# Computing neighbouring output tiles in pairs, with their matmuls in alternating PSUM banks, in a transformer forward pass on one core

## The reference

```python
def conv_ffn(h, w_up, conv_w, conv_b, w_down):
    u = h @ w_up                      # 1024 -> 2 x 2816
    up = jnp.pad(u, ((0, 0), (CONV_W - 1, 0), (0, 0)))
    c = conv_b + sum(up[:, j:j + Tp] * conv_w[j] for j in range(CONV_W))
    gate, val = jnp.split(c, 2, axis=-1)
    return (jax.nn.silu(gate) * val) @ w_down

def sq_relu_mlp(hn, w1, w2):          # 1024 -> 4096 -> 1024
    return jnp.square(jax.nn.relu(hn @ w1)) @ w2
```

## Time and profile before

| what | value |
|---|---|
| median of 3 runs | 1442.1 us (1436.69 to 1442.25) |
| the profiled execution: span | 1441.2 us |
| TensorE busy | 1380.6 us (96%), 10268 matmuls |
| VectorE busy | 925.0 us (64%) |
| ScalarE busy | 662.0 us (46%) |
| GpSimd busy | 471.5 us (33%) |
| mean granted TensorE clock | 0.934 |
| share of the chain that ended last on TensorE | 88% |

### The profile page before, as it was taken

The page is one execution under the profiler, slowest core; times in us unless marked ns, Lnnn a source line. Parts: engine busy times, 40 slices in busy tenths (PEclk is TensorE's granted clock), DMA queues, the critical chain, the costliest instruction groups (busy, mean ns, idle before and its releaser), DMA issues.

```text
span 1441.2 us, 29845 instructions
## 1 busy us (share of the span) xinstructions
PE 1380.6 (96%) x10268; PEld 1311.5 (91%) x10268; DVE 925.0 (64%) x1574; ACT 662.0 (46%) x1100; POOL 471.5 (33%) x479
## 2 busy tenths in 40 slices
PE   6899999999999898999999999999999899999997
PEld 5796999999999767999998899999999886999997
DVE  4587479996656665799955587565554663655542
ACT  3334345554443363465643445454434453444432
POOL 4020135553102312355521023278411000488322
PEclk9995799999999867999999999999999986999999
DMA  5740146556554201566565655666667440566662
GB/s 139 226 137 0 55 143 175 173 169 183 170 151 143 74 1 52 146 193 179 172 197 186 198 146 159 177 181 183 183 184 187 119 125 1 147 194 184 193 187 75
DMA packets 404187, 212.09 MB, mean 147 GB/s; under 512 B 21320, under 2 KB 398424, under 8 KB 403968
## 3 DMA queue, kind: packets, MB, share of 16 engines
q1 hardware_dynamic: 402176, 204.36, 49.3%
q0 software_dynamic: 880, 5.00, 1.0%
q10 hardware_dynamic: 1040, 1.50, 0.3%
HBM read 209.74 MB, written 3.23 MB: 148 GB/s over the span
## 4 chain that ended last, share of the span: by engine, by line
PE 88%; DVE 6%; POOL 2%; issue 2%; ACT 1%; DMA 1%; DVEq 0%; ACTq 0%; SPq 0%; POOLq 0%
PE bank L490 24%; PE bank L491 24%; PE bank L492 24%; PE bank L641 3%; PE bank L592 2%; DVE w_lo L1533 2%; PE bank L616 2%; PE bank L587 1%; PE bank L572 1%; PE bank L905 1%; PE bank L907 1%; PE bank L906 1%; DMA w_raw<-in_w_in_a_dram 1%; POOL acc L1386 1%; PE bank L935 0%
## 5 line engine op out<-in xcount | busy, mean ns | idle before, releaser
L1533 DVE TENSOR_TENSOR w_lo<-w_raw,w_hi 128x1024 fp32r<-128x1024 f32 x391 | 480.4, 1241 | 43.2 <-ACT w_hi L1074 42.6
L1074 ACT ACTIVATE w_hi<-w_raw 128x1024 fp32r<-128x1024 f32 x391 | 410.7, 1051 | 179.2 <-PE bank L492 143.6
L490 PE MATMUL bank<-xh,w_lo 128*128 128x256 f32 (+2 forms) x1640 | 477.2, 291 | 10.9 <-DVE xl L1590 7.1
L491 PE MATMUL bank<-xl,w_hi 128*128 128x256 f32 (+2 forms) x1640 | 470.8, 287 | 0.0
L492 PE MATMUL bank<-xh,w_hi 128*128 128x256 f32 (+2 forms) x1640 | 470.3, 287 | 0.0
L490 PE MATMUL bank<-wide_h,w_lo 128*128 128x256 f32 (+1 forms) x1324 | 381.6, 288 | 8.4 <-DVE wide_l L1601 2.0
L492 PE MATMUL bank<-wide_h,w_hi 128*128 128x256 f32 (+1 forms) x1324 | 378.6, 286 | 0.0
L491 PE MATMUL bank<-wide_l,w_hi 128*128 128x256 f32 (+1 forms) x1324 | 378.4, 286 | 0.0
L490 PEld LDWEIGHTS bank<-xh,w_lo 128*128 128x128 f32 x1640 | 313.4, 191 | 14.7 <-DVE xl L1590 8.3
L492 PEld LDWEIGHTS bank<-xh,w_hi 128*128 128x128 f32 x1640 | 313.5, 191 | 0.3
L491 PEld LDWEIGHTS bank<-xl,w_hi 128*128 128x128 f32 x1640 | 313.2, 191 | 0.3
(11 more groups left out here) (245 smaller groups left out, 1386.3 us busy)
## 6 DMA issues: line engine op xcount, KB each, us to landing
w_raw<-in_mlp_w_dram SPq DMA_DIRECT2D x256, 256.0 KB, 3.1
w_raw<-in_w_up_dram SPq DMA_DIRECT2D x176, 256.0 KB, 3.2
w_raw<-in_w_down_dram SPq DMA_DIRECT2D x64, 256.0 KB, 3.3
w_raw<-in_a_w_in_dram SPq DMA_DIRECT2D x64, 256.0 KB, 3.5
w_raw<-in_w_in_a_dram SPq DMA_DIRECT2D x34, 256.0 KB, 4.2
w_raw<-in_w_kv_b_dram SPq DMA_DIRECT2D x32, 256.0 KB, 3.2
w_raw<-in_a_w_out_dram SPq DMA_DIRECT2D x32, 256.0 KB, 3.1
w_raw<-in_w_down_dram SPq DMA_DIRECT2D x32, 192.0 KB, 4.0
```

Source lines behind the costliest of these rows:

```text
L490: pe.matmul(dst, lo, mov_h, start=first, stop=False)
L491: pe.matmul(dst, hi, mov_l, start=False, stop=False)
L1074: act.activation(w_hi[:, n % R, :], w_raw[:, n % R, :], ACT.Copy)\
L1533: dve.tensor_tensor(w_lo[:, n % R, :], w_raw[:, n % R, :], w_hi[:, n % R, :].bitcast(F32), ALU.subtract)\
```

## The change

In the wo, up and mlp stages PE takes two neighbouring tiles together (`two_products`): it waits for both banks and both weight blocks, and then issues for each k-slice L530, L532 and L534 for the one tile and the other in turn, so that two matmuls in a row write different banks. The same 48 matmuls as before are issued for two tiles; both `block_done` come with the last two of them. `stat_sums` goes to the middle of the first pair. On DVE, in loop stages with one block per tile, `prep(g)` comes ahead of `after(g)`. ACT, POOL and SP are left as they were.

```diff
--- before.py
+++ after.py
@@ -512,6 +512,28 @@
                                       k == 0, k == nk - 1)
                         return ins
                     step(s, i, g, b, body)
+
+            def two_products(s, i, g, mh, ml, t0, ready, nk, middle=None):
+
+                slots = [(s.n0 + g + t) % R for t in range(2)]
+                dsts = [stream[(s.t0 + g + t) % R][:, 0:T - t0] for t in range(2)]
+                for t in range(2):
+                    bank_free(s, i, g + t)
+                pe.wait_ge(S["lo_ready"], at(i, 4, s.n0 + g + 2))
+                for k in range(nk):
+                    if i is None:
+                        ready(k)
+                    if k == nk // 2 and middle is not None:
+                        middle()
+                    w = slice(k * P, (k + 1) * P)
+                    for slot, dst in zip(slots, dsts):
+                        pe.matmul(dst, w_lo[:, slot, w], mh(k), start=k == 0, stop=False)
+                    for slot, dst in zip(slots, dsts):
+                        pe.matmul(dst, w_hi[:, slot, w], ml(k), start=False, stop=False)
+                    for slot, dst in zip(slots, dsts):
+                        ins = pe.matmul(dst, w_hi[:, slot, w], mh(k), start=False, stop=k == nk - 1)
+                        if k == nk - 1:
+                            ins.then_inc(S["block_done"], 1)
 
             def from_x(s, t0=0):
                 base = SPLITS[s.name]
@@ -781,18 +803,25 @@
 
             def simple(name, src):
                 s = ST[name]
-                sweep(pe, s, lambda s, i, g: product(s, i, g, **src(s)), peel=True)
+
+                def pair(s, i, g):
+                    if g % 2 == 0:
+                        two_products(s, i, g, **src(s))
+                sweep(pe, s, pair, peel=True)
 
             def up(name, t0, first=None):
                 s = ST[name]
 
-                def group(s, i, g):
-                    product(s, i, g, **from_x(s, t0 if first is None else first))
+                def pair(s, i, g):
+                    middle = None
                     if i is None and g == 0:
-                        stat_sums(NORM[name], t0)
-                    if i is None and g == 1:
+                        middle = lambda: stat_sums(NORM[name], t0)
+                    if g % 2 == 0:
+                        two_products(s, i, g, middle=middle,
+                                     **from_x(s, t0 if first is None else first))
+                    if i is None and g == 0:
                         rb_sums(NORM[name], t0)
-                sweep(pe, s, group, peel=True)
+                sweep(pe, s, pair, peel=True)
 
             def down(name, t0, nk, stride, sem_, base):
                 s = ST[name]
@@ -1539,8 +1568,12 @@
                 def group(s, i, g):
                     for b in range(s.bpg - 1):
                         prep(s, i, g * s.bpg + b)
-                    after(s, i, g)
-                    prep(s, i, (g + 1) * s.bpg - 1)
+                    if s.loop and s.bpg == 1:
+                        prep(s, i, g)
+                        after(s, i, g)
+                    else:
+                        after(s, i, g)
+                        prep(s, i, (g + 1) * s.bpg - 1)
                     if late is not None:
                         late(s, i, g)
                 sweep(dve, ST[name], group, straight=straight)
```

## The result

The changed kernel takes **1559.1 us** (median of 4 executions, 1557.7 to 1563.2), the kernel before 1439.4 (4, 1432.8 to 1442.3). The ratio is 1.0838, 95% interval 1.0792 to 1.0885: slower by 8.4%. The forecast was 1544, the range 1505 to 1600. The profiled execution took 1559.77 us.

The account below looks back on a forecast made before the run. The prediction took PE to set the time before, and a DVE-ACT ring after the change. Terms 61 + 17 + 3 + 2 + 4 + 15 = 102 us on 1442 gave 1544 us, range 1505 to 1600.

Parts of the forecast that it names:

- The bank changes: PE's matmuls in pairs: alternating banks gain nothing; at most 6 ns a step, 25 us in all.
- The ring: Up and mlp stages: u, ACT's work, high half, DVE's low half, next u can't overlap; +61 us up, +17 mlp.
- Its Silu waits for a tap of tile 2 and starts 1.48 after u: Up stages, turn from g = 3: ACT's Silu delays the high half, making the turn 4.03 us.
- The clock: PE gaps in up0 and up1: half clock for 6.8 us behind one gap in four, +15 us.
- The starts: Starts of up0, up1 and mlp1: POOL's sum for `stat_sums` comes late; +1 us each, +3.
- The mlp stages: mlp0 and mlp1: ring turn of 3.11 us a tile against 2.84, 64 tiles, +17 us.
- The wo stages: wo stages: DVE already slower than PE, low half already in that ring; 0, at most +1 us a stage.
- 7 x 1: Rival without change: pipeline fills a tile later in each of seven stages, 1449 us; 4%.
- The ends: Ends of up0 and up1: last gated slice late for the down stage; 0 to +4 us each, +4 in all.
- the clock falls in most passes: Rival, up stages: gaps ahead of second pairs mostly bring half clock, near 1593 us; 15%.
- Faster: Rival, PE's matmuls: alternation cuts the step by 6 ns to 112 ns, 1417 us; 2%.
- No change: Rival: blocks ready anyway, needing ACT's high half ahead of cin; 1449 us; 4%.

Follow-up runs that it names:

- e5: e4 with each tile's three matmuls of a k-slice in a row in one bank; 1457.4 us, 1.0113 times before.
- e4: Changed kernel, pairs kept, with ScalarE making the next high half before its work on u, VectorE the next low half after its own; 1470.0 us, 1.0191 times before.
- e6: Kernel before, one tile at a time, with e4's order on both ScalarE and VectorE; 1413.7 us, 0.9820 times before.
- e9: e4 with the common wait kept, but all 24 matmuls of one tile ahead of the other's, each signalling its own end; 1428.7 us, 0.9912 times before.
- e2: Kernel before, one tile at a time, with only VectorE's new order, low half ahead of u(g); 1539.8 us, 1.0662 times before.
- e8: Changed kernel with eight extra unused matmuls ahead of each pass's second pair in up0 and up1; 1546.9 us, 1.0738 times before.
- e10: The same kernel as e6, timed again; 1420.0 us, 0.9849 times before.
- e1: Changed kernel with VectorE's order as in the kernel before, TensorE still taking pairs; 1664.6 us, 1.1538 times before.
- e3: Changed kernel, pairs and waits kept, with each tile's three matmuls of a k-slice in a row in one bank; 1550.5 us, 1.0758 times before.

## Why the prediction was right, and where it was off

The forecast was 15 us low, with the verdict and the main mechanism right. By its own steps:

**The bank changes gain nothing: right.** The test is e5 against e4, which differ in how often the bank changes and in nothing that PE waits for in mlp: the same time. There is a difference of 1.3 ns a step that the change does bring: four tiles of mlp take 11.36 us before, in e6 and in e9, which is 118.3 ns a matmul, and 11.23 in e4 and e5, 117.0. It comes with taking two tiles slice by slice, not with a bank change at each matmul, and is worth about 1 us in each mlp stage. Its cause isn't shown.

**The ring: right in kind.** The wait that it named is the one that grew, from 43 to 233 us, and e2 and e4 show it from both sides: the order alone makes it, and ScalarE's order alone takes it away. Of its four turns in up0 one was too short:

| turn from | predicted | measured |
|---|---|---|
| g = 0 | 3.41 | 3.43 |
| g = 1 | 3.41 | 3.36 |
| g = 2 | 3.72 | 3.67 |
| g = 3 | 4.03 | 4.67 |

"Its Silu waits for a tap of tile 2 and starts 1.48 after u": it started 1.81 after it (293.94 to 295.75). The Silu took 0.40 to the high half, not 0.31, and the low half, 1.45 long and not 1.23, 1.37 to u, not 1.14. The forecast took a low half that ran in 1.22 us. But before the change too, one low half in each pass of the up stages takes 1.42 to 1.45:

```profile
317.66 1.44 DVE L1533 TENSOR_TENSOR w_lo<-w_raw,w_hi 128x1024 fp32r<-128x1024 f32 x1
```

What makes it longer wasn't tested. POOL's copy to `wide_h` runs beside it (297.77, 1.19 us long), but is not enough by itself: nine other low halves of up0 in the changed kernel have that copy beside them and take 1.22 to 1.23. Ten long ones have the end of POOL's gate product beside them as well. Passes of 15.13 and 14.96 us in place of 14.57 add some 10 us: the ring in the up stages is 11 x (15.13 - 12.11) + 11 x (14.96 - 11.44) = 72 us where the forecast had 61.

**The clock: +15 forecast, 12 measured (e8).** Most stretches are shorter than assumed, 3.4 us of half clock and not 6.8, but they come behind half of the gaps and not one in four.

**The starts: +3 forecast, -4 measured.** Both up stages had lost time at the start before the change too, and now lose less beyond their passes: 5.7 us in up0 and 3.9 in up1 (from e8, where the clock does not add to it), 7.0 in each before. mlp1's start takes 0.3 more. So up0 and up1 cost 79 in all against the forecast's 78: errors that cancel, which is luck.

**The mlp stages: right.** Four turns of 3.08, 3.08, 3.08 and 3.19 are 12.43, predicted 4 x 3.11 = 12.44, which makes 17 us in the two stages as forecast. The rotary angles gave PE a gap of 4.60 us where it was 1.87 (+2.7; +2 was taken).

**The wo stages: wrong, 10.5 us for 0 to 3.** "The low half was in that ring before" holds, and the turns have stayed (3.31 between the two adds below, 3.43 in the earlier trace rows). What was missed is when the turns begin. VectorE's timeline, the first two adds of wo_a after the change, and the first before it:

```profile
169.45 0.44 DVE L1615 TENSOR_TENSOR h<-h,bank 128x272 f32 x1 [7.24 <-PE bank L534]
...
172.76 0.43 DVE L1615 TENSOR_TENSOR h<-h,bank 128x272 f32 x1
```

```profile
164.01 0.44 DVE L1582 TENSOR_TENSOR h<-h,bank 128x272 f32 x1 [5.49 <-PE bank L492]
```

The first add comes 8.95 us after the stage's first matmul (160.50 to 169.45), before it came after 5.24 (158.77 to 164.01): 3.7 us later, and wo_a is 3.7 us longer. The first tile of a pair ends one matmul ahead of the second, so the ring of a stage in which VectorE is the slower one starts a whole tile later, and nothing later makes that up. I had costed that only as a rival, "7 x 1"; the price is about a tile of PE's time, 3.2 us in wo_c. In wo_a and wo_b it is 3.7: they begin at half clock, which lasts 5.9 and 4.7 us into them where it lasted 4.1 and 3.0.

**The ends: 8.5 for 4.** PE ahead of the first matmuls of down0, down1, and behind the angles in mlp0:

```profile
379.61 0.39 PE L490 MATMUL bank<-wide_h,w_lo 128*128 128x272 f32 x1 [2.88 <-POOL wide_l L1438]
...
812.47 0.58 PE L490 MATMUL bank<-wide_h,w_lo 128*128 128x256 f32 x1 [3.41 <-POOL wide_l L1438]
...
1041.09 0.79 PE L530 MATMUL bank<-xh,w_lo 128*128 128x256 f32 x2 [4.60 <-DVE w_lo L1562]
```

The releaser is as predicted (the last gated slice, POOL's `wide_l`). Two gaps of 2.9 and 3.4 us, at the top of "0 to +4 each", and the 5.9 us behind the second run at half clock, which the estimate left out.

Term by term the profiles' 116 us are 72 for the ring in up, 17 in mlp, 11 for the clock, 10.5 in wo, 8.5 at the ends, 3 at mlp0's start and angles, -4 at the other starts and -2 elsewhere. The wo stages, the long turn and the ends are what the forecast lacked, 26 us; the starts, the clock and the untouched stretches gave 13 of them back.

Of the rivals, "the clock falls in most passes" was nearest in kind, but it falls in half of them, and a stretch costs half of what it assumed. "Faster" is ruled out by the steps. "No change" needed ScalarE's high half ahead of its work: e4 gives it just that, and the pairs still cost 1.9%. That rest, the tiles ending together, was in no rival; as long as the ring was there most of it was hidden behind it (e2 shows 98 us for the order alone, the whole change 120).

## What to carry to other kernels

Before you move a preparing instruction ahead of a consuming one on an in-order engine, follow what it waits for: if the other engine makes that only behind work that waits for the first engine's own last output, the move closes a ring, and its turn, not the busy time of any engine, sets the pace. Here it paid when both engines prepared ahead (e6 and e10: 0.7 to 1.0% less at like clocks, 1.5 to 1.8% by the medians), and cost 6.6% when one did (e2). And interleaving two tiles on the engine that sets the pace makes both end late and together, which costs the one that consumes them; waiting for both ahead of time (e9) costs little or nothing.

## What was not expected of the hardware

**The granted clock of a long stretch differs between profiles, in code that no edit touches.** From e10 and then e5, busy time by windows, TensorE alone, inside the third attention section, whose code is the same in both:

```profile
core 0: us, PE busy (x), PEclk, DMA share, GB/s
1167.00:1204.00 37.00, 37.00 (x112) 0.50 0.08 23
```

```profile
1200.00:1220.00 20.00, 19.42 (x107) 1.00 0.01 4
```

In e10, as in the kernel before and most others, 34 to 38 us run at half clock there. In e5 and in e1 that stretch is missing. From kva's first matmul to wo_c's it is 83.9 and 85.2 us in these two and 99 to 103 in eight profiles; e3 and e9 lie between, with 24 and 27 us at half clock and 97.2 and 96.2 in all. A difference of 16 us is of the size by which executions of one kernel differ (e5 1444 to 1461, e6 1412 to 1434), but no kernel was profiled in both kinds, so that this is their cause isn't shown. What decides between the two was not found.

**A gap does not always cost the clock.** Of PE's 18 waits of 2.0 to 2.6 us ahead of a second pair, from the third pass on, 9 are followed by 3.4 us at half clock; those of 0.5 to 0.7 are not. Nor is the length of the wait alone what decides. In e1, 2 of the 9 waits of 2.60 us in up0 were followed by half clock, and all 9 of 2.55 us in up1. Before the change the gap of 1.87 us in mlp0 was not, that of 1.83 in up0 was the earlier trace rows.
